# Even and odd attention heads paired on the tensor engine, in a two-block model on one Trainium2 core

## The reference

```python
# dilated attention: 12 heads, 4 for each of three dilations
s = einsum('nhbqd,nhbkd->nhbqk', qb, kband) * ATT_SCALE
s = where(valid, s + bias, -inf)
m = max(s, -1); p = exp(s - m); l = sum(p, -1)
o = einsum('nhbqk,nhbkd->nhbqd', p / l, vband)
lse = m + log(l)
# the three dilations of an output head are mixed with softmax(lse)

# sparse attention: 8 query heads, one shared key and value head;
# a mask from an index keeps the 64 best keys of each query
```

## Time and profile before

| | |
|---|---|
| time, median of 3 runs | 2842.14 us (2840.62 to 2842.34) |
| span of the profiled execution | 2833.1 us |
| what lies around the span, against the median | 9.0 us |
| busy: PE, PEld, DVE, ACT | 2648.3, 2036.8, 1269.9, 838.0 us |
| chain that ended last | PE 71%, DMA 20%, DVE 5%, ACT 2% |
| HBM read | 681.11 MB |
| mean granted TensorE clock | 0.980 |

### The profile page before, as it was taken

One profiled execution on the slowest core, in us unless ns is written; L12 is line 12 of the kernel. 1 busy time (PEld: TensorE's weight loads), 2 busy tenths in 40 slices (PEclk: granted clock), 3 DMA queues, 4 the chain that ended last, 5 costly groups with the idle time before them and its releaser, 6 DMA issues.

```text
span 2833.1 us, 46156 instructions
## 1 busy us (share of the span) xinstructions
PE 2648.3 (93%) x19543; PEld 2036.8 (72%) x19543; DVE 1269.9 (45%) x1869; ACT 838.0 (30%) x1039; POOL 0.2 (0%) x4
## 2 busy tenths in 40 slices
PE   8899888879899888879999999999999999999998
PEld 8743433348543333369999889999899998899998
DVE  5610110046411000055657756655655667666555
ACT  4300000025210000033343432443433444423433
POOL 0000000000000000000000000000000000000000
PEclk9999999999999999999999999999999999999999
DMA  8689999972799999955563431445555544323553
GB/s 269 256 358 425 426 425 426 425 267 90 311 401 425 425 425 425 426 170 182 196 218 122 133 119 62 135 164 179 179 179 190 186 152 134 105 76 102 167 179 134
DMA packets 286235, 684.65 MB, mean 242 GB/s; under 512 B 11962, under 2 KB 217586, under 8 KB 236660
## 3 DMA queue, kind: packets, MB, share of 16 engines
q1 hardware_dynamic: 282792, 671.27, 63.2%
q10 hardware_dynamic: 3276, 10.93, 1.0%
HBM read 681.11 MB, written 1.05 MB: 241 GB/s over the span
## 4 chain that ended last, share of the span: by engine, by line
PE 71%; DMA 20%; DVE 5%; ACT 2%; issue 1%; DVEq 1%; SPq 0%; ACTq 0%; POOLq 0%
PE psum L419 69%; DMA weight_ring<-in_w_gate 14%; DMA weight_ring<-in_w_up 3%; DMA weight_ring<-in_w_down 2%; PE psum L427 1%; DVE weight_ring_parts L2038 1%; ACT weight_ring_parts L2030 1%; DVEq L552 1%; DVE arena L3230 0%; DMA h_tok<-in_mem 0%; SPq L1893 0%; DVE arena L3256 0%; DVE arena L1809 0%; DMA weight_ring<-in_w_in 0%; DVE arena_parts L2127 0%
## 5 line engine op out<-in xcount | busy, mean ns | idle before, releaser
L419 PE MATMUL psum<-weight_ring_parts,arena_parts 128*128 128x256 f32 (+1 forms) x2992 | 671.5, 317 | 4.9 <-DVE arena_parts L2131 1.9
L2038 DVE TENSOR_TENSOR weight_ring_parts<-weight_ring,weight_ring_parts 128x2048 fp32r<-128x2048 f32 x217 | 496.6, 2291 | 347.1 <-ACT weight_ring_parts L2030 341.1
L419 PE MATMUL psum<-x_chan_parts,weight_ring_parts 128*128 128x256 f32 x3200 | 611.5, 282 | 13.1 <-DVE arena_parts L2127 7.9
L2030 ACT ACTIVATE weight_ring_parts<-weight_ring 128x2048 fp32r<-128x2048 f32 x217 | 414.9, 1913 | 483.3 <-POOLq L532 347.4
L419 PE MATMUL psum<-weight_ring,arena 128*64 128x512 f32 (+1 forms) x2112 | 474.8, 582 | 73.5 <-DMA weight_ring<-in_w_gate 38.9
L419 PEld LDWEIGHTS psum<-weight_ring_parts,arena_parts 128*128 128x128 f32 x2992 | 501.5, 191 | 41.4 <-DVE arena_parts L2131 2.1
L419 PEld LDWEIGHTS psum<-x_chan_parts,weight_ring_parts 128*128 128x128 f32 x3200 | 508.5, 190 | 18.5 <-issue 13.2
L419 PE MATMUL psum<-arena 64*64 64x64 f32 (+7 forms) x4616 | 492.6, 335 | 29.5 <-DVE arena L1809 15.8
L419 PEld LDWEIGHTS psum<-weight_ring,arena 128*64 128x64 f32 (+1 forms) x2112 | 179.3, 140 | 361.1 <-issue 358.2
L419 PEld LDWEIGHTS psum<-arena 64*64 64x64 f32 (+3 forms) x4616 | 261.3, 141 | 237.3 <-issue 210.9
L419 PE MATMUL psum<-weight_ring_parts,x_chan_parts 128*128 128x256 f32 x2336 | 427.8, 285 | 1.6 <-DVE arena_parts L2127 1.6
(11 more groups left out here) (322 smaller groups left out, 1742.9 us busy)
## 6 DMA issues: line engine op xcount, KB each, us to landing
weight_ring<-in_w_gate SPq DMA_DIRECT2D x92, 1024.0 KB, 23.2
weight_ring<-in_w_up SPq DMA_DIRECT2D x92, 1024.0 KB, 22.9
weight_ring<-in_w_in SPq DMA_DIRECT2D x70, 1024.0 KB, 5.2
arena<-in_w_down SPq DMA_DIRECT2D x64, 1024.0 KB, 22.5
weight_ring<-in_w_down SPq DMA_DIRECT2D x64, 1024.0 KB, 23.2
weight_ring<-in_ffa_w_in SPq DMA_DIRECT2D x44, 1024.0 KB, 7.2
weight_ring<-in_ffb_w_in SPq DMA_DIRECT2D x44, 1024.0 KB, 5.6
arena<-in_w_gate SPq DMA_DIRECT2D x36, 1024.0 KB, 18.5
```

The costliest lines, as they stand in the source:

```text
L419: return nc.tensor.matmul(*args, **kw)
L2030: nc.scalar.activation(HIGH[buf], ring[:, sl, :], ACT.Copy).then_inc(s_hi, 1)
L2038: nc.vector.tensor_tensor(ring_parts[:, sl, :], ring[:, sl, :], f32(HIGH[buf]), ALU.subtract).then_inc(s_split, 1)
```

## The change

Heads are handled in pairs (2p, 2p + 1). Two new helpers serve both stages. `pe_score_pair` takes two pieces, waits for both, and issues the matmuls of the even and the odd head in turn. `pe_value_pair` waits for both copies and issues the value matmuls of both heads in turn. The order on TensorE becomes: scores 0,1; the dense block; scores 2,3; then for each pair p the transposes of its two heads, the values of pair p - 1, the scores of pair p + 2. The further blocks of the dilated stage stand after pairs 1 and 2. The transposed probabilities have four buffers, not two. VectorE, ScalarE and GpSimd follow the new list of pieces; in the sparse stage VectorE's read of the dense block now stands before the softmax of head 2, and ScalarE runs two heads of exponentials ahead of the copies, not one.

```diff
-        v_block_at = {2: 1, 5: 2}
+        v_block_at = {1: 1, 2: 2}
+        PTR4 = view(9728, 4, T, SEQ)
+        def pe_score_pair(p, q, k):
+            banks = []
+            for _ in range(2):
+                banks.append(pe.take())
+                pe.e.wait_ge(s_free[banks[-1]], pe.emptied())
+            for t in range(T):
+                for i, h in enumerate((2 * p, 2 * p + 1)):
+                    last = pe.mm(ps[:, banks[i], t * SEQ:(t + 1) * SEQ], q(h)[:, t * P:(t + 1) * P], k(h),
+                                 start=True, stop=True)
+                    if t == T - 1:
+                        last.then_inc(s_full[banks[i]], 1)
+        def pe_value_pair(p, turned, out, val, probs):
+            for n in turned:
+                pe.e.wait_ge(s_free[n % BANKS], pe.read_out(n))
+            for jt in range(T):
+                for h in (2 * p, 2 * p + 1):
+                    last = pe.mm(out(h), val(h, jt), probs[:, h % 4, jt, :], start=(jt == 0), stop=(jt == T - 1))
+            return last
...
-            for h in range(3):
-                score(h)
+            score(0)
             pe_tok(x)
+            v_pieces = [pe.pieces.n - 1]
+            score(1)
             pe.e.wait_ge(s_acc_free, pe.c["accf"].next())
-            v_pieces = [pe.pieces.n - 1]
-            for h in range(DIL_HEADS):
-                n = turned(h)
-                if h:
...
-                    values(h - 1, held)
-                held = n
-                if h + 3 < DIL_HEADS:
-                    score(h + 3)
-                if h in v_block_at:
+            for p in range(DIL_HEADS // 2):
+                turned = [pe_turned(DIL_P[:, h % 4]) for h in (2 * p, 2 * p + 1)]
+                if p:
+                    values(p - 1, held)
+                held = turned
+                if 2 * p + 4 < DIL_HEADS:
+                    score(p + 2)
+                if p in v_block_at:
                     pe_tok(x)
                     v_pieces.append(pe.pieces.n - 1)
...
-        DPRB, DSB, DPTR = lay(DH, T, SEQ), lay(2, T, SEQ), lay(2, T, SEQ)
+        DPRB, DSB, DPTR = lay(DH, T, SEQ), lay(2, T, SEQ), lay(4, T, SEQ)
...
-            for h in range(3):
-                score(h)
+            score(0)
             pe_chan((XH, XLM))
+            score(1)
             pe.e.wait_ge(s_acc_free, pe.c["accf"].next())
-            for h in DHS:
-                n = turned(h)
-                if h:
-                    values(h - 1, before)
-                before = n
-                if h + 3 < DH:
-                    score(h + 3)
-            values(DH - 1, before).then_inc(s_acc_full, 1)
+            for p in range(DH // 2):
+                turned = [pe_turned(DPRB[:, h]) for h in (2 * p, 2 * p + 1)]
+                if p:
+                    values(p - 1, held)
+                held = turned
+                if 2 * p + 4 < DH:
+                    score(p + 2)
+            values(DH // 2 - 1, held).then_inc(s_acc_full, 1)
...
             exponential(0)
-            for h in DHS:
-                if h + 1 < DH:
-                    exponential(h + 1)
...
+            exponential(1)
+            for p in range(DH // 2):
+                for h in (2 * p, 2 * p + 1):
+                    if h + 2 < DH:
+                        exponential(h + 2)
+                    b = s.take()
+                    s.e.wait_ge(s_full[b], s.filled())
+                    nc.scalar.activation(DPTR[:, h % 4], heads2(b), ACT.Copy).then_inc(s_free[b], 1)
+                if 2 * p + 4 < DH:
+                    s.skip(2)
...
-            for h in range(3):
-                softmax_head(h)
+            softmax_head(0)
+            softmax_head(1)
             v_shifted_channels(0)
-            for h in range(3, DH):
-                v.skip()
-                softmax_head(h)
+            softmax_head(2)
+            softmax_head(3)
+            for p in range(2, DH // 2):
+                v.skip(2)
+                softmax_head(2 * p)
+                softmax_head(2 * p + 1)
```

More of the change, by code:

```diff
@@ L1163, in build, with pe_turned @@
         slopes = [float(2.0 ** (-8.0 * (h + 1) / DIL_HEADS)) for h in range(DIL_HEADS)]
-        v_block_at = {2: 1, 5: 2}
+        v_block_at = {1: 1, 2: 2}
[11 more added lines that the diff above has]
+                        last.then_inc(s_full[banks[i]], 1)
+        def pe_turned(probs):
+            pe.e.wait_ge(s_exp, pe.c["exp"].next())
+            pe.transposes([(jt * SEQ + t * P, probs[:, t, jt * P:(jt + 1) * P], P, P)
+                           for jt in range(T) for t in range(T)])
+            return pe.pieces.n - 1
+        def pe_value_pair(p, turned, out, val, probs):
[5 more added lines that the diff above has]
+            return last
         def pe_b():
@@ L1185, in pe_b @@
                 pe.e.wait_ge(s_free[n % BANKS], pe.read_out(n))
[L1187 to L1204, removed]
@@ L1206, in pe_b, with score, values @@
-            for h in range(3):
-                score(h)
+            def score(p):
+                pe_score_pair(p, lambda h: QT[rows_of(h), h // 2, :], lambda h: KT[rows_of(h), h // 2, :])
+            def values(p, turned):
+                if p % 2 == 0:
+                    done = v_pieces[p // 2]
+                    pe.e.wait_ge(s_free[done % BANKS], pe.read_out(done))
+                return pe_value_pair(p, turned,
+                                     lambda h: ps[rows_of(h), 4 + h // DIL_OUT, h % DIL_OUT // 2 * SEQ:(h % DIL_OUT // 2 + 1) * SEQ],
+                                     lambda h, jt: VV[:, jt, h * HD:(h + 1) * HD], PTR4)
@@ L1309, in s_b @@
             copy_piece(s, VV[:, :, 0:BLK])
[L1310 to L1319, removed]
+            s.skip(2)
+            for p in range(DIL_HEADS // 2):
+                for h in (2 * p, 2 * p + 1):
+                    if h + 2 < DIL_HEADS:
+                        exponential(h + 2)
+                    b = s.take()
+                    s.e.wait_ge(s_full[b], s.filled())
+                    nc.scalar.activation(PTR4[:, h % 4], heads2(b), ACT.Copy).then_inc(s_free[b], 1)
+                if 2 * p + 4 < DIL_HEADS:
+                    s.skip(2)
+                if p in v_block_at:
+                    i = v_block_at[p]
                     for _ in range(2 if i == 1 else 1):
@@ L1471, in g_b @@
                 g.freed()
-            g.skip(3)
+            g.skip(2)
             g.freed()
-            for h in range(DIL_HEADS):
-                g.skip(2 if h + 3 < DIL_HEADS else 1)
-                if h in v_block_at:
+            g.skip(2)
+            for p in range(DIL_HEADS // 2):
+                g.skip(4 if 2 * p + 4 < DIL_HEADS else 2)
+                if p in v_block_at:
                     g.freed()
@@ L2651, in pe_sparse, with score, values @@
             pe_merge_retention()
[L2653 to L2669, removed]
-            for h in range(3):
-                score(h)
+            def score(p):
+                pe_score_pair(p, lambda h: DCT[rows_of(h), h // 2, :], dkey)
+            def values(p, turned):
+                return pe_value_pair(p, turned,
+                                     lambda h: ps[rows_of(h), 4 + h // 4, (h // 2 % 2) * SEQ:(h // 2 % 2 + 1) * SEQ],
+                                     lambda h, jt: DTV[:, jt, :], DPTR)
+            score(0)
             pe_chan((XH, XLM))
+            score(1)
             pe.e.wait_ge(s_acc_free, pe.c["accf"].next())
-            for h in DHS:
-                n = turned(h)
-                if h:
-                    values(h - 1, before)
-                before = n
-                if h + 3 < DH:
-                    score(h + 3)
-            values(DH - 1, before).then_inc(s_acc_full, 1)
+            for p in range(DH // 2):
[6 more added lines that the diff above has]
+            values(DH // 2 - 1, held).then_inc(s_acc_full, 1)
             pe_to_heads(RCP_TOK)
@@ L2689, in s_sparse @@
             s_ahead(26)
-            s.skip(4)
+            s.skip(5)
             def exponential(h):
```

31 lines of the change are left out of this document (15 added, 16 removed).

## The result

The changed kernel takes 2827.96 us (median of 15 runs, 2813.57 to 2839.49) and the one before 2839.16 (15 runs, 2830.68 to 2842.34). The ratio is 0.9961 with a 95% interval of 0.9948 to 0.9973: 11 us saved at 2839.16, between 8 and 15. The forecast was 10.4 us saved and a time of 2831.7. That time was worked out from 2842.14, the median of the first three runs of the kernel before; measured against it the changed kernel is 14.2 us under, of which 3.0 belong to the base.

The account below looks back on a forecast made before the run. TensorE's order was taken as the bound in the dilated and sparse heads. Savings of 8.1 + 2.3 = 10.4 us give a span of 2822.7 and, with the fixed 9.0, a time of 2831.7 us; range 2824 to 2840.

Parts of the forecast that it names:

- The side-by-side work (a, b): TensorE, both stages: array halves run together; a pair's scores take 1.14 us, 2.12 before, its values 1.08, 2.00 before.
- The rival without it: Both stages: no side-by-side work beyond what the kernel has; 2.6 us saved, time 2839.5; chance 0.06.
- The walk (d): Dilated heads: new order stepped through with engine durations and waits; last copy ends at 702.76, not 710.89, saving 8.1 us.
- The sparse stages (e): Sparse heads: projections start at 1616.3 against 1617.42, 1.1 us saved per stage, 2.3 for two layers.
- What follows the stages: Expert stage after the dilated heads: as long as its bytes at 425 GB/s, so an earlier start moves it whole.
- The sum: Whole kernel: 8.1 us from the dilated heads plus 2.3 from the sparse stages, 10.4 us saved.
- a remainder of 9.0 us: Whole kernel: profiled span 2833.1 lies 9.0 under the median 2842.14; taken as fixed and added to the span after, 2822.7.
- The clock rival: Three paired stages: TensorE's clock falls, up to 20.4 us lost, 2852; chance 0.05 for three low stretches, 0.04 for fewer.

Follow-up runs that it names:

- kernel 1: Pairs in the dilated heads alone, sparse heads one by one as in the kernel before; 2828.86 us against 2836.64, ratio 0.9970.
- filling: Six gate products moved from the branch's end into two recurrence waits: in the changed kernel 2821.49 us, ratio 0.9937; in the one before 2832.00 against 2836.16.
- the repeats: The changed kernel run again twice, unchanged, beside the kernel before: 2823.25 us, ratio 0.9942, and 2824.19 us, ratio 0.9952.
- kernel 4: The changed kernel with the even head's matmuls issued first, then the odd head's, inside each pair; 2827.85 us, ratio 0.9967 against the kernel before.

## Why the prediction was right

**The side-by-side work (a, b).** Right in mechanism and size: 8 records in 1.13 us where the earlier trace rows gave 1.14, and a pair of heads in one half takes 1.96. The rival without it was put at 2.6 us saved; run for itself it saved nothing: the dilated stage gave 3.0 and not 4.0, and the clock fell in its sparse stages, which the walk did not have. The Trainium skill's rule on weight loads and row groups (TensorE: Matmul & The Clock Gate, Part 3), taken alone, would have made value pairs slow. The trace disagrees: 16 records of values, two pairs of them, start and end within 2.04 us.

**The walk (d).** It said 8.1 us; the stage lost 8.9 (53.8 - 44.9). Measured from the first score, its end of the new order was 40.0 us and the trace has 39.7; its end of the old order 48.1, and the trace 48.6. The old order was walked 0.5 too short and the new one 0.3 too long, and both misses made the gain look smaller. The waits stood where it had put them, 1.49 and 0.91 for 1.4 and 1.05, in the dilated stage, and 0.36, 1.63, 0.91, 0.33, 0.36 and 0.99 for 0.4, 1.8, 1.05, 0.3, 0.5 and 1.2 in the sparse one.

**The sparse stages (e).** Mis-sized, 2.3 for 3.4 us. The walk put values 6,7 22.8 us after the first score, and there they are: their weight loads start at 1602.57, 22.7 after it. The mis-sized term is the tail behind them: 0.94 + 2.18 + 0.17 = 3.3, in the trace 2.8. The 32 broadcasts and the turn take 1603.49 to 1605.37, 1.9 us, where the sum has 2.35. Its price of 0.068 was a busy time of 1.91 for 28 records that runs 0.07 past the start of the projections, so the last record's end and the turn stood in it already, and the turn was added once more; what the rest comes from is open.

**What follows the stages.** Right. DMA stayed at 1.01 and 425 GB/s, and kernel 1 passed the whole of its shorter dilated stage on: 8.9 us shorter, 8.4 under before at equal clock.

**The sum and the clock.** 8.9 + 3.4 = 12.3 us, and 12.5 at equal clock. The measured medians of the first comparison differ by 11. That this is so near to 10.4 is in part luck: the stages gave 1.9 us more than forecast, and that comparison shows 1.3 us less than the level at equal clock. The time of 2831.7 also rested on a remainder of 9.0 us around the span; each run lists 1.8 (2830.59 against 2828.8), and the rest was the distance between one execution and the median of others. The clock rival was put into the three stages, and there no new low stretch came. The one that the trace shows lies in the recurrence behind them and cost 8.7 us in it.

Is it caused by the change? The same recurrence, with the same instructions, kept its clock in 12 of 18 cases in the nine profiles without filling, in the same execution in one layer and not in the other. It took 66.6 us each time that it kept it and 75.3 each time that it fell, and the fall came 45.3 to 45.4 us after the first 64*64 record in all six. The clock's records also show what sets the six apart: the low stretch before, behind the sparse heads, began 53.55 to 53.68 us ahead of the first 64*64 record in the six, and 48.15 to 53.39 ahead in the twelve. So in these profiles it went by how the clock's stretches lay against the work, and not by the instructions alone; why is not shown. Whether pairs in the sparse stage make the fall likelier stays open: the fallen ones all belong to kernels with sparse pairs, 6 of 14 against 0 of 4, which four cases can't carry, and the mean clock over 33 and 69 runs is the same.

The range of 2824 to 2840 held the median of 2827.96. It took the clock as 4 us either way, and single runs lie up to 14 from that median; one of the repeats, at 2823.25, is just below it.

## What to carry to other kernels

Two heads of half the array's width cost TensorE nearly the time of one if their matmuls follow each other in its queue; the order inside the pair was indifferent here. Before pairing, add up the other engines: by the prediction's sum VectorE needs 3.3 us a pair and TensorE 3.24, a pair then took 3.6 to 4.9, and the first pairs waited because a score was issued behind a dense block and not ahead of it. When a kernel's runs spread by more than the change is worth, read the clock's low stretches and compare stage lengths: where the clock stayed up in the dilated stage it took 44.88 to 44.93 us in six profiles whose times run from 2817.67 to 2830.59.

## What the runs showed of the hardware that was not expected

TensorE runs matmuls of two halves side by side though they were not issued in turn: 1.14 us for 8 records in kernel 4. The granted clock fell for 20.5 us in a recurrence of small matmuls in 6 of 18 profiled cases and cost 8.7 us each time; the six differ from the twelve by where the low stretch before them began, 53.55 to 53.68 us ahead of the recurrence and not 48.15 to 53.39. With nine dense matmuls in each of two waits it fell in none of 6 cases. But only in one of these did the stretch before begin in that band, at 53.55, so it is not shown that the filling prevents the fall. And where work stayed in one half of the array, in pairs, the clock fell to 0.52 inside the sparse stage (1597 to 1604), in both layers of the one profile. The cause is open: the kernel before, which takes one head at a time there, kept 1.00, so did the changed kernel with TensorE idle for a sixth of the time, and kernel 4, on both halves, lost it for 3.4 us in one stage.
